# A new memory map for a two-layer mixture-of-experts trunk: six sets of weight buffers, filled from earlier points

## The reference, cut to what matters

```python
def swiglu(x, wg, wu, wd):
    return (jax.nn.silu(x @ wg) * (x @ wu)) @ wd

def moe_ffn(x2d, router, bias, w_gate, w_up, w_down, sh_gate, sh_up, sh_down):
    scores = jax.nn.sigmoid(x2d @ router)           # 64 experts
    ...                                             # 8 experts per token, of the 4 best of 8 groups
    y = lax.map(expert_block, (slot_tok, block_e, slot_gate))   # swiglu(x2d[tok], w_gate[e], w_up[e], w_down[e])
    routed = jax.ops.segment_sum(y, slot_tok, num_segments=T)
    return swiglu(x2d, sh_gate, sh_up, sh_down) + routed
```

## Time and profile before

| What | us |
|---|---|
| Three runs | 1654.01, 1660.28, 1659.56 (median 1659.56) |
| The profiled execution, its own time | 1653.13 |
| Its span, first to last instruction | 1651.4 |
| RWKV: last state step on VectorE | 304.75 |
| First half of the output projection done (TensorE L1748) | 330.87 |
| First gather issued, both layers | 373.67 and 1084.98 |
| Mean granted TensorE clock from 375 to 380 | 0.67 |
| Layer 0's last norm done | 937.0 |
| Attention: last transpose of h (TensorE L1840) | 943.9 |
| Attention: first addition of a projection to the base (VectorE L2775) | 1034.7 |
| Attention: output projection done | 1059.65 |
| A gather or a scatter, issue to landing (median) | 6.7 and 6.5 |
| Before the group ranking (L2591) VectorE waits for GpSimd | 0.26 in each layer |
| Layer 0, sum of the second tile: TensorE waits for its routed rows until | 920.5 |

### The profile page before, as it was taken

One profiled execution on the slowest core, in us unless ns is written; L12 is line 12 of the kernel. 1 busy time (PEld: TensorE's weight loads), 2 busy tenths in 40 slices (PEclk: granted clock), 3 DMA queues, 4 the chain that ended last, 5 costly groups with the idle time before them and its releaser, 6 DMA issues.

```text
span 1651.4 us, 33659 instructions
## 1 busy us (share of the span) xinstructions
PE 1462.9 (89%) x12824; PEld 950.6 (58%) x12824; DVE 615.8 (37%) x1580; ACT 318.4 (19%) x743; POOL 330.2 (20%) x412
## 2 busy tenths in 40 slices
PE   6989988899998888888888798999998888888886
PEld 4776877656665555555554376566655555555542
DVE  5362352672333333333332704533333333333327
ACT  1521332111111111111111015201111111111110
POOL 6012000021222222222221200212222222222210
PEclk9999989899999999999999799989999999999998
DMA  6330002359999999999997961399999999999986
GB/s 199 125 113 1 4 4 80 105 202 383 409 414 414 415 416 415 416 415 414 415 416 307 357 181 52 116 377 397 414 415 415 415 415 415 416 415 416 415 347 246
DMA packets 139862, 508.21 MB, mean 308 GB/s; under 512 B 29273, under 2 KB 58273, under 8 KB 104188
## 3 DMA queue, kind: packets, MB, share of 16 engines
q1 hardware_dynamic: 103312, 456.49, 69.2%
q0 software_dynamic: 22288, 41.89, 7.1%
q10 hardware_dynamic: 14172, 8.54, 1.8%
HBM read 501.38 MB, written 36.90 MB: 326 GB/s over the span
## 4 chain that ended last, share of the span: by engine, by line
PE 42%; SPq 23%; DMA 23%; DVE 6%; issue 3%; POOL 1%; ACT 1%; ACTq 0%; DVEq 0%; POOLq 0%
SPq L844 23%; DMA arena<-in_moe_w_up 21%; PE ps L781 10%; PE ps L1423 6%; PE ps L799 3%; PE ps L1553 3%; PE ps L1865 2%; PE ps L1967 2%; PE ps L762 1%; PE ps L769 1%; DMA arena<-routed 1%; PE ps L1748 1%; PE ps L1006 1%; PE ps L1849 1%; PE ps L1760 1%
## 5 line engine op out<-in xcount | busy, mean ns | idle before, releaser
L781 PE MATMUL ps<-arena 128*64 128x256 f32 x2048 | 234.6, 381 | 57.0 <-DMA arena<-in_moe_w_up 57.0
L781 PE MATMUL ps<-ring,arena 128*64 128x256 f32 x2048 | 234.6, 382 | 51.7 <-DMA ring<-in_moe_w_up 37.7
L774 DVE COPY arena<-ps 128x512 f32<-128x512 f32 x128 | 88.6, 692 | 512.3 <-PE ps L769 512.3
L781 PEld LDWEIGHTS ps<-arena 128*64 128x64 f32 x2048 | 163.6, 137 | 151.1 <-issue 106.2
L818 POOL DMA_INDIRECT arena<-hrows,arena x128 | 129.4, 1011 | 584.2 <-DVE arena L814 570.3
L781 PEld LDWEIGHTS ps<-ring,arena 128*64 128x64 f32 x2048 | 154.6, 137 | 153.5 <-issue 78.7
L823 POOL DMA_INDIRECT routed<-arena x128 | 117.9, 921 | 240.3 <-DVE arena L942 175.9
L942 DVE TENSOR_SCALAR arena<-ps,arena 64x512 f32<-64x512 f32 x128 | 95.1, 743 | 162.2 <-PE ps L799 162.2
L896 ACT COPY arena<-ps 128x256 f32<-128x256 f32 x128 | 47.6, 372 | 536.7 <-PE ps L781 536.7
L906 ACT ACTIVATE arena<-ps,arena 64x512 f32<-64x512 f32 x128 | 87.5, 683 | 206.0 <-PE ps L799 206.0
L799 PE MATMUL ps<-ring,arena 128*64 128x512 f32 x512 | 124.0, 605 | 0.0
(11 more groups left out here) (375 smaller groups left out, 1577.4 us busy)
## 6 DMA issues: line engine op xcount, KB each, us to landing
ring<-in_moe_w_gate SPq DMA_DIRECT2D x64, 1024.0 KB, 24.4
ring<-in_moe_w_up SPq DMA_DIRECT2D x64, 1024.0 KB, 24.7
ring<-in_moe_w_down SPq DMA_DIRECT2D x64, 1024.0 KB, 24.1
arena<-in_moe_w_gate SPq DMA_DIRECT2D x64, 1024.0 KB, 24.8
arena<-in_moe_w_up SPq DMA_DIRECT2D x64, 1024.0 KB, 24.3
arena<-in_moe_w_down SPq DMA_DIRECT2D x64, 1024.0 KB, 23.8
arena<-routed SPq DMA_DIRECT2D x16, 1024.0 KB, 14.5
ring<-in_attn_w_qkv SPq DMA_DIRECT2D x6, 1024.0 KB, 16.1
```

The costliest lines, as they stand in the source:

```text
L774: return nc.vector.tensor_copy(xgT.rearrange("p (r j) m -> p j r m", r=2), ps[:, bU, :].rearrange("p (j r m) -> p j r m", j=4, r=2))
L781: mm = nc.tensor.matmul(dst[SLOTS * j:SLOTS * j + SLOTS, 0:FF], xgT[:, k, :], slot_of(s + j)[:, FF * k:FF * k + FF], start=(k == 0), stop= ...
```

## The change

The arena grows by 2908 columns and everything in it is placed anew; helper tables of RWKV move into it, the residual sums are made in h itself and not in accumulators. There are now 18 slots, six sets, used in the order ORDER. Loads at a stage's entry are issued by `sp_enter` at named points and no longer in one place: in layer 0 eleven slots from the last state step on VectorE, in layer 1 six from the end of layer 0's last norm, behind the loads of the attention weights for queries, keys and values and ahead of those for the output. The last three slots lie where the shared gate and up and the turned h lie, and are freed by su1. The shared expert's sg1 and half of su1 now come ahead of expert 0 in place of the dummy matmuls, the rest behind it; its down projection comes behind experts 1 to 3, and its down matrix, loaded in routing, lies where the LayerNorm rows lay, which are loaded behind expert 7. The gather buffers are no longer cleared. Scatter buffers are two instead of four, index buffers twelve instead of eight. Eight experts stand before the loop, twelve in it, eight behind it.

```diff
-UNROLL = 8
-HEAD = 5
-TAIL = 3
-ARENA = 30956
-SETS = 4
+UNROLL = 12
+HEAD = 8
+TAIL = 8
+ARENA = 33864
+SETS = 6
+ORDER = (2, 3, 6, 7, 8, 9, 10, 11, 12, 13, 14, 4, 5, 0, 1, 15, 16, 17)
+INDICES = 12
...
         def plan_experts(l):
-            for s in range(RING, 3 * SETS):
-                slot_free[s] = (rv if l == 0 else av).end()
+            if l == 0:
+                for slot in range(RING, 15):
+                    slot_free[slot] = rv.at(f"y_{NCH - 1}")
+            else:
+                for slot in range(RING, 12):
+                    slot_free[slot] = end_dve[0].end()
+                for slot in (12, 13):
+                    slot_free[slot] = av.at("add4")
+                slot_free[14] = av.at(f"add{LAST}")
+            for slot in (15, 16, 17):
+                slot_free[slot] = moe_pe[l].at("su1")
...
-            n += 1
-        for q in range(4):
-            plan("attn", f"ao{q}", n % RING, [(slot3(n % RING), w_nat(I["attn_w_o"][0], 256 * q, 256))],
-                 ap.at("o0_1"))
-            n += 1
+        for q, slot in zip(range(4), (4, 5, 0, 1)):
+            plan("ao", f"ao{q}", slot, [(slot3(slot), w_nat(I["attn_w_o"][0], 256 * q, 256))],
+                 ap.at("o0_0" if q < 2 else "o0_1"))
...
+        def sp_enter(sp, L, l, *places):
+
+            for i in places:
+                if L.entry_free[ORDER[i]]:
+                    sp.wait_ge(*L.entry_free[ORDER[i]])
+                sp_fetch(sp, l, (0, i // 3), i % 3)
...
+        def mm_shared_down(pe, l, u):
+
+            r0, n = TILES[u // 2]
+            if u >= 2:
+                pe.wait_ge(*moe_dve[l].at("sd", u - 2))
+            for j in range(2):
+                m = nc.tensor.matmul(ps[0:n, bS[u % 2], :], shm[:, j, r0:r0 + n],
+                                     shared_w[2][:, D * j + 512 * (u % 2):][:, 0:512], start=(j == 0), stop=(j == 1))
+            m.then_inc(*moe_pe[l].step("sd", u))
+
         def pe_experts(pe, L, l):
...
-            keep_busy(SPARE_BANK[1], 4)
+            pe.wait_ge(*moe_act[l].at("sg0"))
+            mm_shared(pe, l, "sg1", range(KC))
+            pe.wait_ge(*moe_dve[l].at("sm0"))
+            mm_shared(pe, l, "su1", range(KC // 2))
             pe_turn_x(pe, L, l, (0, 0))
 
             def body(e):
                 pe_expert(pe, L, l, e)
                 if early(e, 0):
-                    pe.wait_ge(*moe_act[l].at("sg0"))
-                if early(e, 2):
-                    pe.wait_ge(*moe_dve[l].at("sm0"))
-                if isinstance(e[0], int) and e[1] < 4:
-                    mm_shared(pe, l, ("sg1", "su1")[e[1] // 2], range(KC // 2 * (e[1] % 2), KC // 2 * (e[1] % 2) + KC // 2))
+                    mm_shared(pe, l, "su1", range(KC // 2, KC))
+                if early(e, 1):
+                    pe.wait_ge(*moe_dve[l].at("sm1"))
+                    pe.wait_ge(shared_loaded[2], 16 * (l + 1))
+                if isinstance(e[0], int) and 1 <= e[1] <= 3:
+                    for u in (2 * e[1] - 2, 2 * e[1] - 1):
+                        mm_shared_down(pe, l, u)
...
+                if early(e, HEAD - 1):
+                    pool.wait_ge(*moe_pe[l].at("sd"))
+                    load_ln(pool, I["ln_ffn_g"][l], I["ln_ffn_b"][l])
...
             for l in range(2):
-                sp.wait_ge(*(rp.at(f"y_{NCH - 1}") if l == 0 else av.at(f"neg{LAST}")))
-                for j, w in enumerate((I["shared_w_gate"], I["shared_w_up"])):
-                    sp.dma_start(shared_w[j], w[l].rearrange("(p k) n -> p (k n)", k=KC)).then_inc(shared_loaded[j], 16)
                 set_main(l)
+                if l == 0:
+                    sp_enter(sp, main, l, *range(11))
+                    shared(l, 0, rv.at("res0_2"))
+                    sp_enter(sp, main, l, 11, 12)
+                    shared(l, 1, rp.at("o1_1"))
+                    sp_enter(sp, main, l, 13, 14)
+                else:
+                    static("qkv")
+                    sp_enter(sp, main, l, *range(2, 8))
+                    static("ao")
+                    sp_enter(sp, main, l, 0, 1, 8, 9, 10)
+                    shared(l, 0, ap.at(f"sc{LAST}"))
+                    shared(l, 1, ap.at(f"pv{LAST}"))
+                    sp_enter(sp, main, l, 11, 12, 13, 14)
+                sp_enter(sp, main, l, 15, 16, 17)
                 sp_experts(sp, main, l)
...
-                load_ln(I["ln_ffn_g"][l], I["ln_ffn_b"][l])
-                for b in range(4):
-                    nc.gpsimd.memset(xs[b], 0.0).then_inc(cleared, 1)
...
+                    pool.wait_ge(*ap.at("hT"))
                     pool.wait_ge(attn_loaded, 16 * 4)
...
-                pe.wait_ge(*moe_dve[l].at("sm1"))
-                pe.wait_ge(shared_loaded[2], 16 * (l + 1))
-                pe.wait_ge(main.index, main.base + E)
-                for u in range(6):
-                    r0, n = TILES[u // 2]
-                    for j in range(2):
-                        m = mm_(ps[0:n, SD_BANKS[u], :], shm[:, j, r0:r0 + n],
-                                shared_w[2][:, D * j + 512 * (u % 2):][:, 0:512], start=(j == 0), stop=(j == 1))
-                    m.then_inc(*st.step("sd", u))
...
+                act.wait_ge(*prev_dve.end())
+                act.dma_start(shared_w[2], I["shared_w_down"][l].rearrange("(p j) n -> p (j n)", j=2))\
+                    .then_inc(shared_loaded[2], 16)
```

310 lines of the change are left out of this document (148 added, 162 removed).

## The result

| | Kernel before | Changed kernel |
|---|---|---|
| Median, same chip (7 runs each) | 1660.19 us (1654.01 to 1662.73) | 1642.52 us (1637.55 to 1649.18) |
| Profiled execution, its own time | 1653.13 | 1638.70 |
| Its span | 1651.4 | 1637.0 |

The ratio is 0.9889, 95% interval 0.9865 to 0.9913: faster by 1.1%, more than the 0.5% that a measurement can tell. The forecast was 1646.0 us in 1633 to 1660. On the scale of the profiled execution it was -13.4 us; measured -14.4.

A forecast was written before the change was run, and what follows sets the result against it. The DMA stream was taken to bound the experts: bytes left once loading resumes. Terms -4.5 - 4.3 - 3.0 - 2.0 + 0.4 = -13.4 us took the profiled 1653.1 to 1639.7; scaled to the median, 1646 us, range 1633 to 1660.

The forecast's parts named there:

- main term: Expert weight stream: fewer bytes left when loads resume, though later; last landings 4.5 and 4.3 us earlier in the two layers.
- slow start: Stream just after loads resume: TensorE's pace no longer starves the DMA engines; 1.5 us gained per layer, bounds 0 and 1.9.
- The resumption: When SyncE can load weights without a pause, at su1's end: 5.6 us later in layer 0, 5.8 in layer 1.
- The shared down projection ... hidden by the DMA-bound stage: Experts 1 to 3: its 2.4 us per expert cost nothing, TensorE having 6.8 us spare in every 50.
- Six sets in the steady state: 0 us: Experts past 450 us: DMA engines are already full with four sets, so more sets only lengthen the stock; 0 us.
- the same loss added to 24 x 0.239: Shared matmuls before expert 0: the dummies' clock loss, 1.73 and 2.22 us, added to 5.7 gives 7.5 and 8.0 us.
- Rival A: Before expert 0: all 24 real matmuls at half clock last 11.5 us; only -5.9 us, 1653.6; chance 0.18.
- The bias rows: Attention's start, layer 1: six weight loads beside the bias loads hold ScalarE at most 15.2 us longer; cost 0, 4 us spare.
- Rival B: Attention's start: weight loads dragged to 151 GB/s hold ScalarE 41.7 us longer; kernel 9 us slower, 1668.6; chance 0.09.
- The tail of layer 1: Layer 1's end: without the shared down projection there, the 16-row sum starts earlier; -2 us, bounds 0.9 and 4.
- Rival C: Expert stage: early loads fail to shift the stream, loading resumes another 5 us later per layer; -3.4 us, 1656; chance 0.13.
- Rival D: Whole kernel, more than forecast: full clock at once and no tail loss; -19 us, 1640.5; chance 0.10.

The follow-up runs named there:

- Late entry: Changed kernel, six sets kept, with all fifteen entry loads held until behind the output projection in both layers; 1649.97 us, 0.9925 of the kernel before.
- four sets: Changed kernel with the early load points kept but the two further sets taken away (12 slots); 1671.83 us, 1.0069 of the kernel before.
- gate first: Changed kernel with expert 6's gate and up issued ahead of the three loads that wait for su1; 1641.09 us, 0.987 of the kernel before.

## Why the prediction was right, and where it was not

**The number and its main term were right.** Fewer bytes behind resumption, and resumption later: the last landings came 490.9 us after resumption in both layers, against 491.9 and 491.4 less 1.5 for the slow start. Late entry measured the worth of the early points by themselves, 3.8 us per layer by the first profile and 2.8 by the second; four sets showed that without the further sets nothing of the gain is left. That the sum came within 1 us is in part luck. The resumption was 2.8 us better than forecast in the two layers together, and the untouched RWKV stage gave 0.9; against that the stream gave 1.5 us less, the tails 0.8 less, attention took 0.8, and the 0.4 for small edits cannot be seen. The second execution of the changed kernel has a span of 1640.1 us, 11.3 and not 14.4 below the kernel before. The Trainium skill's 358 GB/s ("DMA: Bandwidth & Descriptors", Specifications) would have made 11.7 us per layer out of the bytes alone; measured were 11.1 and 10.6 with 2.0 of slow start in them, and the 415 GB/s that the stream holds over stretches of 50 us decide against it.

**The step that was wrong in its reason: "The shared down projection ... hidden by the DMA-bound stage".** I took the cover to be the later stage's 6.8 us in 50. In experts 1 to 3 there is no such spare time: TensorE is busy all 50 us until 550. The cover is the stock of sets. While the down projection runs, slots come free every 10.7 us against 8.24 of need, and where that starved the stream, the later stretches show 412 to 415 GB/s and no more, so nothing was regained. The price that I set without the cover, 7 us per layer for the down projection alone, was of the right size: with four sets the place of all the shared work costs 3.9 and 7.4 us by the distances and 5.0 by the stream's loss. Going back to four sets as a whole costs 13.0 and 15.2 us per layer (554.6 - 541.6, 557.9 - 542.7), and the kernel is slower than before. My expectation for four sets, 1647 to 1651, came from the same step. "Six sets in the steady state: 0 us" holds; "more sets only lengthen the stock" is true and was taken too lightly, for the stock is what carries nearly the first 200 us.

**"The slow start of the stream"** was taken as 1.5 us per layer, bounds 0 and 1.9. The loss in the first 60 us fell from 3.3 to 1.3, by 2.0 in both layers. With the bytes' 10.1 that makes 12.1, and measured were 11.1 and 10.6; where the other 1.0 and 1.5 us went, no run shows.

**The resumption: right in kind, off in size, and not a constant.** Against the kernel before it moved by +4.6 and +4.0 us in the first profile (forecast +5.6 and +5.8), +7.2 and +4.3 in the second. The step "the same loss added to 24 x 0.239" fixed a clock loss that varies: 7.35 us in one execution, 8.55 in the other. Rival A, the cold start, is this mechanism; it did not go to the end (11.5 us), but part of it is there in five of the nine profiles whose code is the same up to expert 0 of layer 0 (31.3 to 32.4 us from the norm instead of 29.8). That SyncE's order is what delays the resumption behind expert 0 was right: gate first moved it by 3.4 and 4.7 us.

**The bias rows: right that they cost about nothing, wrong on the margin.** The term was 15.2 us at most for ScalarE's hold, with 4 us to spare before ScalarE's limit of 979.8. Measured 19.9 us (43.3 - 23.4): 4.7 over my upper bound, which took the six loads to be served once at 415 GB/s. One issue alone took 15.42. Shifted by layer 0's earlier end (-7.1 us) the limit was 972.7, and ScalarE came at 973.2. Attention lost 0.8 us in this execution. In the second the hold was 41.4 us, ScalarE came at 975.1, 1.4 us within its limit there, and attention lost nothing. Rival B, 41.7 us more, falls. The Trainium skill's rule that I set against it ("DMA: Bandwidth & Descriptors", Queues, rings and completion order: each engine takes turns between its queues packet by packet) is not refuted by a hold of 20 us, but my reading of it, that the large packets are soon through and 15 us is the most, is.

**The tail of layer 1.** Forecast -2, bounds 0.9 and 4; measured -1.4 from the last landing. (The prediction's "46.5 us, not 48.5" for that distance was misread: by its own landmarks it is 1651.4 - 1599.78 = 51.6 before, and it is 50.2 now.) The shared down's departure gave what it should: the 16-row matmuls now wait for the rows alone. But TensorE, without work before them, runs them at the lower clock and they take 3.58 us, where 1.83 would do; this was in the text as a reason for the lower bound. Layer 0: +0.2, forecast 0.

**Rival C** (the stream is not shifted) falls by the landings. **Rival D** had the whole clock at once and no tail loss; neither came.

**Small edits and the steady state.** +0.4 was forecast for routing; between norm and the first pick no difference above the clock's spread can be told.

## What to carry to other kernels

Where a stream of loads bounds a stage as it does here, its end is the time at which loading resumes without a pause, plus the bytes left, plus every gap in which too few free buffers were at hand; so price work that is moved in among the first consumers by the period at which it frees buffers against the stream's own, and by how many loads are already asked for. On a queue that issues in order, put the load whose buffer is free first ahead of those that are not. And compare single executions by distances inside a stage: here the untouched start differed by 5 us and more between them, as much as the largest terms.

## What the runs showed of the hardware that I had not expected

- **Issue time on one queue depends on what another has outstanding.** Five issues of small-packet bias loads took 13.61 us alone and 33.95 us beside six loads of 1 MiB. With the six held back they took 13.34. The bound from bytes and rate, 15.2 us more, was too low by 4.7.
- **TensorE's clock fell at different points of the same code.** Two executions had 0.78 and 0.50 of full clock in the same 5 us, and reached expert 0 of layer 0 up to 2.6 us apart. In the tail, the engine had been without work for 1.73 us before 18 dummy instructions, and they ran at 0.44 us each at full clock; after 2.14 us without work fourteen began at 0.53 of full clock and took 0.57 each on average. These are single executions; whether the longer wait is what made the difference, they do not show.
- **A DMA stream that starved did not catch up.** With four sets the rate behind the starved stretch is the same 412 to 415 GB/s as in the other kernels. The place of shared work that costs the stream 11.3 us of its first 60 with four sets costs it 1.3 with six.
